# Two mixers' modulation sums on TensorE, a folded norm, and seven expert weights loaded ahead, in a kernel of two stacked transformer blocks

## The reference

```python
cond = jax.nn.silu(c)
for l in range(2):
    mod = cond @ w_ada[l] + b_ada[l]
    shift1, scale1, gate1, shift2, scale2, gate2 = jnp.split(mod[:, None, :], 6, axis=-1)
    h = x * (1 + scale1) + shift1
    y = token_mixer(h, w_in[l], ...)
    x = layer_norm(ALPHA * x + gate1 * y, ln1_g[l], ln1_b[l])
    h = x * (1 + scale2) + shift2
    y = moe_ffn(h, ...)
    x = layer_norm(ALPHA * x + gate2 * y, ln2_g[l], ln2_b[l])
```

## Time and profile before

| | before |
|---|---|
| runs, us | 3000.75, 3000.25, 2990.05 |
| median | 3000.25 us |
| the profiled execution | 2994.28 us, span 2992.5 us |
| TensorE matmul busy | 2798.5 us (94%) |
| VectorE, ScalarE, GpSimd busy | 1629.0, 756.6, 409.8 us |
| chain that ended last | TensorE 74%, VectorE 12%, DMA 9% |
| traffic | 718.31 MB, mean 240 GB/s |

### The profile page before, as it was taken

How to read it: one execution, slowest core, us unless ns; L and a number is a source line. 1 busy time by engine, 2 the same in 40 slices (tenths; PEclk the granted TensorE clock), 3 DMA queues, 4 the chain that set the end, 5 groups by cost and what they waited for, 6 DMA issues and landing times.

```text
span 2992.5 us, 65346 instructions
## 1 busy us (share of the span) xinstructions
PE 2798.5 (94%) x27418; PEld 2077.7 (69%) x27418; DVE 1629.0 (54%) x2821; ACT 756.6 (25%) x1400; POOL 409.8 (14%) x343
## 2 busy tenths in 40 slices
PE   7999999988899999999989899999998999899998
PEld 6878566655587866655557588844577887888973
DVE  6745433333473554444436478788757536555555
ACT  0122212121112133323213422200045414443210
POOL 1000000000000000000000036400014302434630
PEclk9999999999999999999999999999999999999999
DMA  9945999999984599999974035485430023000443
GB/s 392 389 161 219 406 405 415 386 421 420 389 365 141 205 381 420 419 407 420 420 310 141 15 113 171 168 308 197 154 106 18 4 82 129 18 16 33 157 167 112
DMA packets 102704, 718.31 MB, mean 240 GB/s; under 512 B 11680, under 2 KB 11968, under 8 KB 18176
## 3 DMA queue, kind: packets, MB, share of 16 engines
...
...
## 4 chain that ended last, share of the span: by engine, by line
PE 74%; DVE 12%; DMA 9%; ACT 2%; issue 2%; SPq 0%; POOL 0%; DVEq 0%; ACTq 0%; POOLq 0%
PE ps L229 16%; PE ps L1614 10%; PE ps L2167 9%; PE ps L2192 7%; DMA arena<-in_w_up 6%; DVE arena L162 6%; PE ps L3139 5%; PE ps L1643 5%; PE ps L2832 3%; PE ps L1705 2%; ACT arena L145 2%; DMA arena<-in_w_down 2%; DVE arena L166 2%; PE ps L2559 1%; PE ps L3571 1%
## 5 line engine op out<-in xcount | busy, mean ns | idle before, releaser
L145 ACT ACTIVATE arena<-ps 128x512 f32<-128x512 f32 (+3 forms) x529 | 266.9, 505 | 1268.0 <-PE ps L229 244.7
L229 PE MATMUL ps<-arena 128*128 128x256 f32 x2144 | 480.1, 385 | 18.5 <-DMA arena<-in_w_in 4.9
L162 POOL TENSOR_TENSOR arena<-arena 128x512 f32<-128x512 f32 (+1 forms) x288 | 376.4, 1307 | 821.7 <-DVE arena L162 284.4
L229 PEld LDWEIGHTS ps<-arena 128*128 128x128 f32 x2144 | 408.7, 192 | 87.1 <-issue 9.7
L1614 PE MATMUL ps<-arena 128*32 128x256 f32 (+2 forms) x5120 | 390.8, 389 | 42.0 <-DMA arena<-in_w_up 31.0
L1614 PEld LDWEIGHTS ps<-arena 128*32 128x32 f32 (+2 forms) x5120 | 248.5, 120 | 187.4 <-issue 87.8
L162 DVE TENSOR_TENSOR arena<-ps,arena 128x256 f32<-128x256 f32 (+3 forms) x416 | 203.8, 490 | 235.0 <-PE ps L3139 87.9
L162 DVE TENSOR_TENSOR arena<-arena 128x512 f32<-128x512 f32 (+6 forms) x473 | 294.1, 622 | 60.7 <-PE ps L2192 35.7
L2167 PE MATMUL ps<-arena 128*128 128x256 f32 (+1 forms) x1792 | 298.5, 328 | 2.2 <-DVE arena L162 1.5
L2192 PE MATMUL ps<-arena 128*128 128x512 f32 x672 | 293.0, 593 | 2.4 <-DVE arena L162 2.2
L2167 PEld LDWEIGHTS ps<-arena 128*128 128x128 f32 x1792 | 270.0, 191 | 29.6 <-DVE arena L171 3.3
...
## 6 DMA issues: line engine op xcount, KB each, us to landing
arena<-in_w_gate SPq DMA_DIRECT2D x128, 1024.0 KB, 13.0
arena<-in_w_up SPq DMA_DIRECT2D x128, 1024.0 KB, 14.1
arena<-in_w_down SPq DMA_DIRECT2D x128, 1024.0 KB, 13.5
...
```

What stands on the lines that cost most here:

```text
L145: self.e.activation(out, in_, func, bias=bias, scale=scale, **more).then_inc(*self.done(key))
L162: self.e.tensor_tensor(out, a, b, op).then_inc(*self.done(key))
L229: ins = pe.matmul(out, a, b, start=start and i == 0, stop=stop and i == len(pairs) - 1)
```

## The change

It has four parts. First, which steps carry the pieces of later vectors, and where their sums stand:

```diff
+        PIECES_AT = ((1, 1, 2, 2, 1, 1, 2, 2, 2, 2, 2, 2, 2, 2, 0), (2, 2, 2, 2, 1, 1, 2, 2, 2, 0, 0, 0, 0, 0, 0))
+        VECTORS_AT = ({4: 2, 6: 3, 8: 4, 10: 5, 12: 6, 14: 7}, {3: 8, 5: 9, 8: 10, 10: 11})
...
-            first = 4 * FROM[l] + 2 * i
-            return range(first, min(first + 2, 4 * FROM[l + 1]))
+            first = 4 * FROM[l] + sum(PIECES_AT[l][:i])
...
 
-            u = FROM[l] + (i - 3) // 2
-            return [u] if i > 2 and i % 2 and u < FROM[l + 1] else []
```

```diff
+                for j in range(4):
+                    ins = pe.matmul(b[32 * j:32 * j + 32, 0:256], ones[:, 0:32], a[:, j * 256:j * 256 + 256], start=True, stop=True)
             ins.then_inc(*made(("mod sums", u)))
...
+            if q == 0:
...
+            reach(pe, *at["silu"])
+            reach(pe, *at["mod piece", n])
+            for k in (2 * q, 2 * q + 1):
+                f = cond[:, k:k + 1]
+                by = bass.AP(f.tensor, f.offset, [list(f.ap[0]), [0, 32]])
+                for j in range(4):
+                    o = k % 2 * 1024 + j * 256
+                    ins = pe.matmul(psum.of["mod sums", u, 0][32 * j:32 * j + 32, 0:256], by, w[:, o:o + 256], start=k == 0, stop=k == 7)
...
+            freed(pe, old)
+            reach(pe, *at["mod stage", u])
+            for c in range(2):
+                o = u % 2 * 256 + c * 128
+                ins = pe.transpose(b[:, c * 128:c * 128 + 128], stage[:, o:o + 128], ident[:, :])
+            ins.then_inc(*made(("mod turned", u)))
 
...
+            o = l * 32 + {0: 0, 1: 1, 3: 2, 4: 3}[v] * 8
+            bias = VO[f"b_ada{l}"] + o - l * 32
+            dve.wait_ge(*at["mod turned", u])
+            do.stt(mod1[:, o:o + 8].rearrange("p (j c) -> p j c", c=2),
+                   psum.of["mod turned", u][:, 0:256].rearrange("p (c j r) -> p j c r", c=2, j=4)[:, :, :, 0],
+                   1.0 if v in (1, 4) else 0.0, vecs[:, bias:bias + 8].rearrange("p (j c) -> p j c", c=2), ALU.add, ALU.add,
```

```diff
+        def first_product(pe, l, out, pairs_of):
+
+            for n, k in enumerate((0, 2, 1, 3, 4, 6, 5, 7)):
+                reach(pe, *at["turned out", l, 0, k])
+                ins = pe.matmul(out, *pairs_of(k), start=n == 0, stop=n == 7)
+            return ins
...
+
+            rstd, shift = (LN[n][:, i:i + 1] for n in (2, 3))
+            dve.wait_ge(*at["ln root", key, i])
+            do.rcp(rstd, rstd)
+            do.ts(shift, LN[1][:, i, 0:1], rstd, -1.0, ALU.mult, ALU.mult, ("ln factors", key, i))
...
+
+            dst = XS[:, t * 1024 + h * 512:t * 1024 + h * 512 + 512]
+            do.fma(dst, psum.tiles[ACC + t * 2 + h][:, :], LN[2][:, t:t + 1], LN[3][:, t:t + 1], ("ln", ("moe", l), t, h))
...
+            shift, scale, both_ = mod1[:, 32:40], mod1[:, 40:48], small[:, 132:140]
+            do.tt(both_, vec("ln2b0"), scale, ALU.mult)
+            do.tt(shift, shift, both_, ALU.add)
+            do.tt(scale, scale, vec("ln2g0"), ALU.mult)
```

Second, in the mixer rope comes earlier on VectorE (and ScalarE takes its root between the value gates of steps 4 and 5), and the memory is carved anew:

```diff
-            modulations(3, 4, 5, 6, 7)
+            modulations(3, 4)
             dve.wait_ge(*at["mixer", l])
             rope_dve(dve, do, ("mixer", l), M.q4, M.t4, 2, 10, M.g3, M.tb[:, 0], M.tb[:, 1], pairs)
             do.cp(M.TM[:, 0:512].rearrange("p (t g r d) -> p t g r d", t=2, g=2, r=2), bc(M.q4[:, :, 8:10, :], 3, 2),
                   ("roped", l))
+            modulations(5, 6, 7, 8)
...
-            modulations(8, 9, 10, 11, 12, 13)
+            modulations(9, 10, 11, 12, 13, 14, 15)
...
+            if l:
+                dve.wait_ge(*at["ln2 rows"])
+                for t in range(2):
+                    f = slice(t * 1024, t * 1024 + 1024)
+                    do.tt(XS[:, f], XS[:, f], M.norms[:, 0:1024], ALU.mult)
+                    do.tt(XS[:, f], XS[:, f], M.norms[:, 1024:2048], ALU.add)
+            else:
+                folded(do)
```

Third, seven pieces of the MoE (shared gate, gate and up of group 0, gate of group 1) are issued right behind the first piece of w_out, once the mixer's last head's values are out, into slots 5 to 11:

```diff
                 load(sp, ("w_bb", l, hf), ("y", l, hf * 4 + 3), D["w_bb"][l, hf])
-            for i in range(4):
+            load(sp, ("w_out", l, 0), ("mixed", l, 0, 1), D["w_out"][l, 0])
+            for i in range(NRING + NAPART, NRING + NEXTRA):
+                weights.used[i] = [(("mixer", l), "values", 3, 0)]
+            load_apart(sp, NRING, ("ws_gate", l), ("shared gate", l), D["ws_gate"][l])
+            for i, (name, r, e) in enumerate(FRONT):
+                load_apart(sp, NRING + 1 + i, (name, l, e), (name[2:], l, r), expert_rows(sp, name, l, e))
+            for i in range(1, 4):
                 load(sp, ("w_out", l, i), ("mixed", l, i, 1), D["w_out"][l, i])
```

`moe_sp` then starts with down of group 0 and up of group 1. Since gate of group 1 lies in memory of the context work, the loads of ctx (layer 0) and of the kept rows (layer 1, 1 MB of the context's queries) wait for `gate(1)`, on SP, and the context work moves to later rounds:

```diff
-        PIECE_ROUNDS = {1: [("rows", 0), ("rows", 1), ("rows", 2)], 2: [("rows", 3), ("qkv", 4)], 3: [("keys", 0), ("keys", 1)],
-                        6: [("qkv", 5)], 7: [("qkv", 0)], 9: [("queries", 0)], 10: [("qkv", 1)], 12: [("queries", 1)], 15: [("qkv", 2)],
-                        16: [("queries", 2)], 17: [("qkv", 3)], 18: [("queries", 3)]}
+        PIECE_ROUNDS = {4: [("rows", 0), ("rows", 1), ("rows", 2)], 5: [("rows", 3), ("qkv", 4)], 6: [("keys", 0), ("keys", 1)],
+                        8: [("qkv", 5)], 9: [("qkv", 0)], 10: [("queries", 0)], 12: [("qkv", 1)], 13: [("queries", 1)],
+                        15: [("qkv", 2)], 16: [("queries", 2)], 17: [("qkv", 3)], 18: [("queries", 3)]}
         HEAD_ROUNDS = {}
-        for a, p in enumerate((1, 3, 7, 10, 14, 16, 18, 21)):
-            q = {3: 6, 7: 9, 10: 12}.get(p, p + 1)
+        for a, p in enumerate((2, 4, 7, 10, 14, 16, 18, 21)):
+            q = {4: 6, 7: 9, 10: 12}.get(p, p + 1)
...
         def moe_sp(sp, l):
-            weights.size, weights.turn, weights.fresh = NRING + EXTRA[l], NRING, ("mixer", l)
-            load(sp, ("ws_gate", l), ("shared gate", l), D["ws_gate"][l])
+            weights.size, weights.turn = NRING + EXTRA[l], 0
             for p, new, _, _ in rounds(l):
...
-                        sp.dma_start(rw, kept[:, 3072:3584]).then_inc(*tables["rows"]("c values kept", 16))
-                if new is not None:
+                if new is not None and new > 1:
                     for e in places_of(new):
                         load(sp, ("w_gate", l, e), ("gate", l, new), expert_rows(sp, "w_gate", l, e))
+                if new == 2 and l:
+                    sp.wait_ge(*at["c kept"])
+                    sp.dma_start(gates[:, 0:1024], kept[:, 2048:3072]).then_inc(*tables["rows"](None, 16))
+                    sp.wait_ge(*at["scores", l])
+                    sp.dma_start(rw, kept[:, 3072:3584]).then_inc(*tables["rows"]("c values kept", 16))
+                    sp.wait_ge(*at["gate", l, 1])
+                    sp.dma_start(CX.rows, kept[:, 0:2048]).then_inc(*tables["rows"]("c queries kept", 16))
+                if new == 4 and not l:
+                    sp.wait_ge(*at["gate", l, 1])
+                    sp.dma_start(CX.rv, D["ctx"].rearrange("(t p) n -> p t n", p=128)).then_inc(*tables["rows"]("rows", 16))
                 early_sp(sp, l, p, (0,))
                 if p >= 0:
                     for e in places_of(p):
                         load(sp, ("w_down", l, e), ("yd", l, p, 1), expert_rows(sp, "w_down", l, e))
-                if new is not None:
+                if new:
```

```diff
+                def last_add(nh):
+                    reach(pe, *at["yf", l, p, nh])
+                    for t in range(2):
+                        pe.matmul(psum.tiles[ACC + t * 2 + nh][:, :], f32(E.ST[p % 2][:, t * 128:t * 128 + 128]),
+                                  E.YF[:, nh * 512:nh * 512 + 512], start=False, stop=True).then_inc(*made(("last added", l, nh, t)))
...
                 early_act(act, do, l, p, 2)
+                if p == 3 and not l:
+                    act.wait_ge(*at["gate", l, 1])
+                    context_rows_act(act, do)
             ln_act(act, do, ("moe", l))
+            for t in range(2):
+                act.wait_ge(*at["ln factors", ("moe", l), t])
+                normed_half(do, l, t, 1)
...
+            for k in (2 * k2, 2 * k2 + 1):
+                do.fma(B.xv[:, k, :], psum.of["columns", 0, k2][:, k % 2 * 256:k % 2 * 256 + 256], vec("ln2g1")[:, k:k + 1],
+                       vec("ln2b1")[:, k:k + 1], ("columns out", 0, k2) if k % 2 else None)
```

220 lines of the change are left out of this document (125 added, 95 removed).

## The result

Over 20 runs each, side by side on one chip, the changed kernel takes 3000.22 us (2990.42 to 3008.32) and the kernel before 2995.38 (2985.41 to 3002.12). The ratio is 1.0019, 95% interval 1.0011 to 1.0028: slower by 3 to 8 us. I had forecast 3 us faster, inside "no change that can be told". The time lies in the range, but with twenty runs of each the difference is clear of noise, and it has the other sign.

The account below looks back on a forecast made before the run. TensorE's work and idle bound the kernel, in places transfers. Terms -8 - 9 - 1 + 9 + 6 = -3 gave 2991 us from the profiled 2994.28, 2997 from the median 3000.25; forecast 2993, range 2968 to 3009.

Parts of the forecast that it names:

- no change that can be told: Whole kernel: a time difference inside about 0.5%, 15 us; chance 0.56.
- Entry: Start of mixer 0: first projection group ends near 35.5 instead of 39.95 us, -4.5 (-6 to -2).
- too few keep-warm matmuls: Rival: first groups at both mixers' starts run at half rate, 3.5 us lost twice, +7, 3000 us; chance 0.08.
- Sums in mixer 0: Four vectors of columns get cheaper on TensorE, -1.1 us each, -4.5; mixer 0 in all -8 (-14 to -4).
- Mixer 1: Two vectors of columns, -1.1 us each; with the end of MoE 0, heads start 9 us earlier (-12 to -6).
- End of MoE 0: Last additions 1.5 us shorter (booked with the MoE), chain behind statistics -5 to -5.5, chunkwise first group 1.4 more.
- the attention (layer 1): Same change ahead of layer 1's attention: -2, its turned-out chunks with a factor +1, together -1 us.
- MoE 0: Layer 0's MoE: round 4 2.5 us earlier, moved context work +12.5, last additions -1.5; +9 (0 to +13).
- The first rival: The MoEs lose nothing: moved context work adds no time, load stream uses the relief; -18, 2976 or 2982 us; chance 0.22.
- No wait for w_out: Mixers: early loads delay w_out 1 to 3 by 17.5 us, but TensorE needs it some 40 us later; no cost.
- MoE 1: Layer 1's MoE: SP's wait for gate 1 delays the load stream, up of group 4 six later; +6 (0 to +9).
- The slower rival: Mixer 0 gains nothing as VectorE is late at six sums, MoEs pay fully; +16.5, 3010 us or more; chance 0.12.

Follow-up runs that it names:

- turned-later kernel: Changed kernel with the sums of columns turned one projection step after they are summed, sums at shifted steps: 2983.47 us, ratio 0.9963 to the kernel before.
- the kernel with the heads late: Changed kernel with layer 1's MoE as before, except the context's first two heads stay in later rounds 2 and 4: 2998.24 us, ratio 1.0015 to before.

## Why the prediction was wrong, by its steps

The step that failed is the price of the sums of later vectors in the two mixers: TensorE's waits for VectorE behind the moved rope. In mixer 0 they were worked out and not added, in mixer 1 not looked at. The forecast gave the two stretches -18 us and they had -3.5.

**Entry: right.** The first group starts 5.3 us earlier; 4.5 was forecast. In the working a group of the projection was taken for eight rows where it has sixteen (3.6 us, not 1.8), since a float32 matmul leaves two; both kernels have it, so it fell out, and the first group ends at 36.6 and not at 35.5. L646 took 3.69 and 3.68 us, so the rival of too few keep-warm matmuls falls.

**Sums in mixer 0: this step failed.** The working has the sums behind rope late by 2.7 and 1.4 us, but its sum, -4.5 - 4.5 + 1, leaves these 4.1 us out; the return named for them, that rope is out of the way of the heads, had no figure, and in the kernel before TensorE went from the projection into the heads (161.28) without a wait (timeline, TensorE, before):

```profile
150.84 10.61 PE L229 MATMUL ps<-arena 128*128 128x256 f32 x48
```

Measured: 3.88 and 1.14 us of waits, and 2.6 more for the half-rate group behind the first. The stretch to the heads gained 2.6 us instead of 8; with the hand-overs a step apart it gained 11. That the later transfers have slack was right: with the waits gone TensorE waits for no transfer behind step 3.

**Mixer 1: this is the step that failed most.** "Two vectors of columns, -1.1 each" was all that the forecast said of its sums; that the same rope stands before VectorE's copy there, and TensorE's transposes behind the copy, was worked out for mixer 0 alone. It costs 7.18 us of wait and some 1.4 of half rate. Forecast for round 25 to the heads: -10; measured: -0.9; with the hand-overs a step later -10.2 (124.2). The gain forecast was there, and was given back at one wait.

**End of MoE 0: right** (5.5 us earlier from the last additions' start to the first group), though made otherwise: the four float32 additions of 512 columns take 3.70 us and not the 1.8 booked (the same slip, rows for matmuls), 1.6 more than the eight rounded ones before, which eats the wait of 1.66 that went; the chain behind them is shorter by 7. For the attention (layer 1) it is 25.9 us from the additions' start to the second product instead of 24.1, +1.7 where -1 was forecast.

**MoE 0: right in the main, 2 us short.** Round 4 was forecast 2.5 us earlier against round 0, measured 2.5; round 10 was forecast 10 later, measured 12.4. The wait for the context's norm was 2.97 and not 1.5, and the one half-rate product of before, which was to go, became four. The mark that the first weights bring next to nothing held within 4 us. The first rival, in which moved work costs nothing because transfers had slack, falls: undoing the move gave the 12 us back. No wait for w_out shows behind the early loads in either mixer, as forecast.

**MoE 1: right** (+6 forecast, +6.7 measured). w_down goes out behind TensorE's gate, and up of group 4 starts 68.1 us behind round 0 instead of 61.6.

**The second block: not in the forecast at all.** No line of it changes, and I gave it nothing beyond the attention's 1. It came out 5.7 us shorter, 5 of them by the slot in which its pieces fall.

That the time fell into the range was luck in part: the mixers brought 14.5 us less than forecast, the MoEs cost 3.1 us more, and 4.8 us in the stretches from the heads to round 0 and 4.7 in the second block that the forecast didn't have made up for more than half of it.

**The slower rival** had the right parts: VectorE late for TensorE at the sums in mixer 0, and MoEs that pay. It put 2 to 3 us at each of six sums where three waits in two mixers made up 12 us and their half-rate groups 4. It said +16.5 where the spans differ by +5. Of the 11.5 between them 5.7 are the last stretch and 4.8 those from the heads to round 0; the mixers, which it gave -10 with the attention, were 6.5 worse, and the MoEs with their cold products, which it gave +26.5, were 7.4 better. By the bound of 0.5% the change is "no change", which had 0.56.

**The half rate behind waits.** The Trainium skill's section "HAM oscillation — how this bites in real kernels", on its page "TensorE: Matmul & The Clock Gate", would have put the sum at +2 by the estimate in the prediction, nearer to +5 than mine. The traces agree in part. In MoE 0 of the changed kernel the products behind idle times of 2.98, 4.25 and 2.12 us took 5.35, 5.34 and 5.35 us, 1.7 more than at the full clock; others went on at 3.66, as behind 2.29 and 2.34 us before and behind 2.91 us in the turned-later kernel. The same product at the last norm took 5.37 us behind a wait of 3.06, and 3.74 behind 3.04 in the kernel with the heads late. So the length of a wait did not tell here whether the product behind it was slow, and the number of slow products is worth some us from kernel to kernel.
